# Final norm's sums and spreads among the queries' units, and five weight tiles' bounds as TensorE sums, in a fused two-block kernel

## The chip, the cores and the metric

One core of a Trainium2 chip runs the whole program in one launch. The metric is the device time of that core in microseconds (us). The kernel before takes 2531.79 us, the median of three runs from 2530.01 to 2536.81.

## The reference

The input `x` has 1024 tokens of 1024 features. A first block adds a gated mixer and a feed-forward part, and ends in a norm. A second block has differential attention, whose queries, keys, values and gates come from one projection of the normed `x`, and then a stick-breaking attention. Around the change it is this:

```python
        h = rms_norm(x, norm2_g[l])
        f = jnp.square(jax.nn.relu(jnp.einsum('bsd,df->bsf', h, w_ff1[l])))
        x = x + jnp.einsum('bsf,fd->bsd', f, w_ff2[l])
    return rms_norm(x, final_g)                       # end of the first block
...
    h = _rms(x, norm_g)                               # a_norm_2, start of the second
    proj = h @ w_in
    q, k, v, g = jnp.split(proj, [DA_QK, 2 * DA_QK, 2 * DA_QK + DA_V], axis=-1)
    qs = [_rope_partial(_rms(q[:, :, :, c], q_norm), pos) for c in range(2)]
    ks = [_rope_partial(_rms(k[:, :, :, c], k_norm), pos) for c in range(2)]
```

## The kernel before, in words

**Numbers.** Every big product is made of three float16 products (high half by high half, high by low, low by high). So every weight tile and every activation is first scaled by a power of two and split into a float16 high half and a float16 low half. The power of two comes from a bound on the tile's values.

**Weight tiles.** Tiles are numbered 0 to 41 (`TILES`). 20 and 21 are the last of the second feed-forward matrix, 22 and 23 the query columns, 24 and 25 the key columns, 26 and 27 the values, 28 and 29 the gates, 30 and 31 the output projection. A tile goes through six steps: a DMA on the SyncE queue lands it in the one raw buffer (`load(i)`, which waits until tile i-1 has been converted, `weight`); VectorE takes each partition's largest magnitude (`measure`, a reduce over 4096 elements, signal `w_peak`); GpSimd reduces that over the partitions (`across`, a `partition_all_reduce`, signal `w_top`); VectorE makes the power of two (`factor`, three tiny instructions by way of `power`, signal `w_factor`); ScalarE writes the high half (`convert`, signal `w_high`); VectorE writes the low half (`convert_low`, signal `weight`). Which step of which tile is put behind which product is written out by hand in two tables, `MEASURE[(tile in use, use)]` and `CONVERT[(tile in use, use)]`; `LOW` is one use behind `CONVERT`. `feed(i, use)` on each engine looks them up.

**Order.** Nothing is scheduled by a tool: five functions (`tensor`, `vector`, `scalar`, `gpsimd`, `sync`) write out the program of each engine in order, and semaphores tie them together. An engine's instruction that waits holds up all that stands behind it on that engine. PSUM has eight banks that `banks.take` deals out in turn, so a new bank waits until the one taken eight takes before has been emptied.

**The end of the feed-forward part.** `ff_end[2]` holds 16 products ("down" products, j = 0 to 15, 12 matmuls each). They add to the second half of the tokens (n = 1; for j = 8 to 15 this is each feature block's last addition). Behind each, VectorE adds the result to the residual, ScalarE squares it twice (once plain, once times `final_g`), and GpSimd adds the squares up (`add_square`, two adds a block).

**The two norms in one.** The final norm and `a_norm_2` follow each other. For each half n of the tokens TensorE sums the squares (`sums("final", n)`), VectorE and ScalarE make the roots (`final_factors`, `final_roots`), VectorE builds a 128 x 512 matrix of four diagonals (`diagonal`), and TensorE multiplies ones by it, which spreads a row of factors over all partitions (`spread`). There are two spreads a half: `a_norm_2` makes the normed input `h` of the projection (`final_h`, which must be there before a product of that half), `final_g` scales the residual in place (`final_x`, wanted only much later: ScalarE's `spill` writes the residual to DRAM, and that must be done before unit 16 can write over it). All diagonals share one buffer, so each waits for the spread before it.

**The queries' and keys' units.** `qk_units` are 32 units of 24 matmuls: u = 0 to 3 are tile 22 for tokens 0 to 3, 4 to 7 tile 23, 8 to 11 tile 22 for tokens 4 to 7, 12 to 15 tile 23, 16 to 23 tile 24, 24 to 31 tile 25. Per unit, ScalarE squares the product (`qk_square`), VectorE reduces, scales and norms it (`qk_norm`, four instructions), GpSimd rotates it (four instructions, signal `rotated`), and TensorE transposes the rotated unit u-3 behind the product of unit u (`qk_turn`); ScalarE and VectorE then split it (`qk_high`, `qk_low`). After the 32 units come 16 products for the values (tiles 26, 27) and 16 for the gates (28, 29).

Every instruction's line number is that of a thin wrapper (`Program`): L72 is a matmul, L75 a transpose, L81 an activation, L84 a copy on ScalarE, L93 a `tensor_tensor`, L96 a `tensor_scalar`, L101 a `scalar_tensor_tensor`, L110 a `tensor_reduce`, L113 a reciprocal, L122 GpSimd's reduce over partitions, L78 a DMA. Buffers: R are the activations, RG the raw tile and the halves of three weight tiles, PS is PSUM, dg the diagonals, scl the small columns of bounds and factors, OV and oss the squares and sums of a query unit.

## Time and profile before

| what | value |
|---|---|
| median of three runs | 2531.79 us |
| the profiled execution's own time | 2530.41 us |
| its span | 2528.6 us |
| TensorE busy | 2363.5 us, 93% of the span |
| VectorE, ScalarE, GpSimd busy | 60%, 38%, 9% |
| mean granted TensorE clock | 0.974 |
| chain that ended last, by engine | PE 76%, DVE 13%, ACT 6%, issue 3% |

The span runs from the first to the last instruction; the execution's own time has 1.8 us around it. TensorE is busy in nearly all of the span, so what a change can win is in its idle stretches. In rows, PE is TensorE's matmul, DVE VectorE, ACT ScalarE, POOL GpSimd and SPq the SyncE DMA queue. In a timeline each row has a start, a duration, the engine, line and operation, the output and inputs, and in brackets how long the engine sat idle before it and who ended that.

### The profile page before, as it was taken

The page shows a single profiled execution, that of the slowest core. Times are in us where ns is not written, and L with a number is a line of the kernel's source. Part 1 is how long each engine was busy: PE and PEld are TensorE (multiplying, and loading weights), DVE is VectorE, ACT ScalarE, POOL GpSimd, SP SyncE. Part 2 cuts the span into 40 slices and gives each one's busy share as a digit, 9 for nine tenths or more (in the row PEclk, how much of TensorE's full clock was granted, in tenths as well). Part 3 has the DMA queues.
Part 4 walks back from the last instruction along what each step waited for, and adds up shares of the span by engine and source line. Part 5 has one row for each costly group of instructions (what it writes and reads, how often), then busy time and mean ns, then how long its engine had stood idle before and what let it go on. Part 6 is the DMA issues. An engine that isn't in the chain of part 4 may idle for free.

```text
span 2528.6 us, 30214 instructions
## 1 busy us (share of the span) xinstructions
PE 2363.5 (93%) x12840; PEld 1252.4 (50%) x12840; DVE 1519.4 (60%) x1962; ACT 968.2 (38%) x1383; POOL 216.0 (9%) x263
## 2 busy tenths in 40 slices
PE   6999999999999999898999777899999998888899
PEld 4445444444444444344444455654444445666764
DVE  6898755644454455777631488965534307888862
ACT  5245334212121212323321466732323116777741
POOL 0001030000000002324201101022000000000000
PEclk9999999999999999898999899999999998999999
DMA  4010011110101010121011000021130100000021
GB/s 177 34 67 34 1 34 63 70 67 34 67 34 67 34 67 34 36 101 67 34 67 34 1 1 1 8 93 34 67 133 34 68 1 34 1 1 1 1 84 50
DMA packets 50326, 116.00 MB, mean 46 GB/s; under 512 B 2386, under 2 KB 7819, under 8 KB 49808
## 3 DMA queue, kind: packets, MB, share of 16 engines
q1 hardware_dynamic: 48456, 105.40, 11.8%
q10 hardware_dynamic: 1736, 8.68, 0.8%
q8 instruction: 101, 1.65, 0.3%
q14 instruction: 33, 0.27, 0.0%
HBM read 101.49 MB, written 12.58 MB: 45 GB/s over the span
## 4 chain that ended last, share of the span: by engine, by line
PE 76%; DVE 13%; ACT 6%; issue 3%; DMA 1%; POOL 1%; ACTq 0%; DVEq 0%; POOLq 0%
PE PS L72 72%; ACT RG L81 4%; PE PS L75 3%; DVE R L93 2%; DVE R L101 2%; DVE RG L107 2%; DVE mx L110 2%; DVE RG L101 2%; ACT OV L84 1%; DVE scl L110 1%; DMA RG<-in_a_w_in 1%; DVE RG L93 1%; DVE oss L110 1%; ACT R L81 1%; ACT OV L81 0%
## 5 line engine op out<-in xcount | busy, mean ns | idle before, releaser
L72 PE MATMUL PS<-R,RG 128*128 128x512 f16 (+1 forms) x5472 | 1167.6, 375 | 10.2 <-DVE RG L101 4.7
L72 PEld LDWEIGHTS PS<-R,RG 128*128 128x128 f16 (+1 forms) x5472 | 543.4, 103 | 631.8 <-issue 14.5
L72 PE MATMUL PS<-RG,R 128*128 128x512 f16 x2880 | 634.6, 381 | 4.5 <-DVE R L101 4.0
L72 PEld LDWEIGHTS PS<-RG,R 128*128 128x128 f16 x2880 | 282.7, 98 | 337.8 <-issue 7.5
L81 ACT ACTIVATE R<-PS,scl 128x512 f32<-128x512 f32 (+1 forms) x192 | 126.8, 687 | 716.1 <-PE PS L72 616.3
L101 DVE SCALAR_TENSOR_TENSOR R<-PS,scl,R 128x512 f32<-128x512 f32 (+1 forms) x208 | 148.7, 746 | 149.2 <-PE PS L72 124.1
L107 DVE TENSOR_TENSOR_SCAN RG<-RG 128x127 f32<-128x127 f32 (+7 forms) x128 | 168.6, 1345 | 110.4 <-ACT RG L81 110.1
L72 PE MATMUL PS<-R,OV 128*128 128x64 f32 (+2 forms) x1456 | 194.5, 286 | 34.9 <-DVE R L93 32.8
L101 DVE SCALAR_TENSOR_TENSOR RG<-RG,scl 128x4096 f16<-128x4096 f32 (+1 forms) x43 | 188.7, 4389 | 52.2 <-ACT RG L81 52.2
L72 PEld LDWEIGHTS PS<-R,OV 128*128 128x128 f32 x1456 | 180.6, 199 | 45.1 <-DVE R L93 39.3
L75 PE MATMUL PS<-ident,RG 128*128 128x128 f32 x864 | 148.5, 289 | 47.1 <-ACT OV L84 23.9
L81 ACT ACTIVATE RG<-RG,scl 128x4096 f16<-128x4096 f32 (+1 forms) x43 | 156.0, 3627 | 94.4 <-DVE scl L113 94.4
L110 DVE TENSOR_REDUCE scl<-RG 128x1 f32<-128x4096 f32 x35 | 154.4, 4413 | 62.1 <-DMA RG<-in_a_w_in 24.6
L122 POOL PARTITION_ALL_REDUCE scl<-scl x62 | 38.8, 628 | 1642.6 <-DVE scl L110 1327.8
L72 PE MATMUL PS<-R 64*128 64x512 f16 (+4 forms) x1216 | 156.7, 363 | 22.3 <-ACT RG L81 20.4
L81 ACT ACTIVATE RG<-PS,scl 128x1024 f32<-128x1024 f32 (+3 forms) x172 | 168.9, 983 | 1.8 <-PE PS L72 1.8
L104 DVE CUSTOM_DVE_ANT_0 R<-R 128x512 f32<-128x512 f32 (+1 forms) x66 | 44.3, 676 | 182.5 <-ACT R L81 182.4
L84 ACT COPY OV<-PS 128x512 f32<-128x512 f32 (+3 forms) x215 | 111.0, 516 | 109.7 <-PE PS L75 105.9
L75 PEld LDWEIGHTS PS<-ident,RG 128*128 128x128 f32 x864 | 103.0, 153 | 61.0 <-DVE RG L101 26.2
L101 DVE SCALAR_TENSOR_TENSOR R<-R,OV 128x1024 f32<-128x1024 f32 x104 | 129.3, 1278 | 1.1
L81 ACT ACTIVATE RG<-PS,mx,scl 128x128 f32<-128x128 f32 (+7 forms) x128 | 106.1, 839 | 41.5 <-DVE mx L96 40.8
L93 DVE TENSOR_TENSOR R<-PS,R 128x512 f32<-128x512 f32 (+1 forms) x96 | 65.3, 683 | 75.4 <-ACT R L81 46.0
(120 smaller groups left out, 1546.7 us busy)
## 6 DMA issues: line engine op xcount, KB each, us to landing
RG<-in_w_ff SPq DMA_DIRECT2D x16, 2048.0 KB, 8.1
RG<-in_a_w_in SPq DMA_DIRECT2D x8, 2048.0 KB, 8.5
RG<-in_w_in SPq DMA_DIRECT2D x4, 2048.0 KB, 9.6
xspill<-R ACTq DMA_DIRECT2D x2, 4096.0 KB, 15.3
RG<-in_w_kv SPq DMA_DIRECT2D x4, 2048.0 KB, 8.0
RG<-in_b_w_in SPq DMA_DIRECT2D x4, 2048.0 KB, 7.9
R<-in_x SPq DMA_DIRECT2D x8, 512.0 KB, 9.1
RG<-in_w_out SPq DMA_DIRECT2D x2, 2048.0 KB, 7.7
```

The lines of the kernel that those rows point to most:

```text
L72: return self.engine.matmul(*a, **k) if self.engine else Nothing()
L75: return self.engine.transpose(*a) if self.engine else Nothing()
L81: return self.engine.activation(*a, **k) if self.engine else Nothing()
L84: return self.engine.copy(*a) if self.engine else Nothing()
L93: return self.engine.tensor_tensor(*a) if self.engine else Nothing()
L101: return self.engine.scalar_tensor_tensor(out=out, in0=in0, scalar=scalar, in1=in1, op0=op0, op1=op1)
L104: return self.engine.tensor_tensor_reduce(*a) if self.engine else Nothing()
L107: return self.engine.tensor_tensor_scan(*a) if self.engine else Nothing()
L110: return self.engine.tensor_reduce(*a, **k) if self.engine else Nothing()
L122: return self.engine.partition_all_reduce(*a) if self.engine else Nothing()
```

## The change

1. For the first half of the tokens, the `final_g` diagonal, its spread and `final_x` leave the last down products (j = 11 to 13) and go to the queries' units 4 (diagonal), 6 (spread), 7 and 8 (`final_x`).
2. For the second half, the sums of squares move from unit 1 to 2, the `a_norm_2` spread from 2 to 3, `final_h` from units 2 and 3 (four blocks each) to 3 to 6 (two each), the `final_g` diagonal from 4 to 8, its spread from 6 to 10, `final_x` from 6, 7 to 10, 11, and the spill from 9 to 12.
3. The hand-written tables change: tile 23 is converted behind down product j = 12 instead of 8; 24 is measured behind unit 9 (before: 5) and its factor made behind 12 (6); 25 is measured behind 17 (10), factor 19 (12); 26 behind 22 (16), factor 24 (17); 27 behind 27 (24), factor 29 (25); 28 behind the values' products 1 and 3 (before 0 and 1). Low halves follow one unit later.
4. For tiles 24, 25, 26, 27 and 30, GpSimd no longer reduces the bound over the partitions. Instead TensorE multiplies a 128 x 128 matrix of ones by the column of peaks (`bound`), which leaves their sum on every partition. It takes a PSUM bank, which the first instruction of `factor` reads and frees. On TensorE the `bound` stands ahead of the product of the unit behind which VectorE makes the factor.

```diff
-for _i in (7, 8, 19, 20, 21, 22, 23, 30, 31, 32, 33, 35):
+for _i in (7, 8, 19, 20, 21, 22, 23, 24, 25, 26, 30, 31, 32, 33, 35):
     del MEASURE[_i, 1], CONVERT[_i, 2]
...
-                   (21, (19, 1), (19, 2)), (22, (19, 6), (20, 1)), (23, (20, 7), (21, 9)),
-                   (24, (23, 2), (23, 3)), (25, (22, 7), (23, 5)), (32, (30, 7), (30, 8)),
+                   (21, (19, 1), (19, 2)), (22, (19, 6), (20, 1)), (23, (20, 7), (21, 13)),
+                   (24, (22, 6), (23, 5)), (25, (24, 2), (24, 4)), (26, (24, 7), (25, 1)),
+                   (27, (25, 4), (25, 6)), (28, (26, 2), (26, 4)), (32, (30, 7), (30, 8)),
...
+BOUNDED = (24, 25, 26, 27, 30)
...
+            def bound(i):
+                b = banks.take(("bound", i))
+                e.wait_ge(*sig("w_peak").at(i))
+                e.wait_ge(*banks.free(("bound", i)))
+                e.matmul(b[:, 0:1], ones[:, :], w_col(i, 0), start=True, stop=True).then_inc(*full.up("bound", i))
+            def feed(i, use):
+                if CONVERT.get((i, use)) in BOUNDED:
+                    bound(CONVERT[i, use])
...
                 if j == 8:
                     spread("a_norm_2", 0)
-                if j == 12:
-                    spread("final_g", 0)
...
             for u, (which, c, t) in enumerate(qk_units):
-                if u == 1:
+                if u == 2:
                     sums("final", 1)
-                if u == 2:
+                if u == 3:
                     spread("a_norm_2", 1)
-                if u == 6:
-                    spread("final_g", 1)
+                if u in (6, 10):
+                    spread("final_g", u // 10)
+                feed(22 + 2 * which + c, t + 1)
                 product_n(22 + 2 * which + c, t, ("qk", u), ready=h_ready("a_norm_2", t // 4))
...
             for t in range(NT):
+                if t == 2:
+                    bound(30)
                 for c in range(2):
                     product_n(28 + c, t, ("gg", t, c))
...
             def factor(i):
+                if i in BOUNDED:
+                    key = ("bound", i)
+                    e.wait_ge(*full.at(*key))
+                    power(w_inv(i), w_col(i, 2), banks.ap(key)[:, 0:1], key=key).then_inc(*sig("w_factor").up(i))
+                    return
...
             for u in range(32):
-                if u == 1:
+                if u == 2:
                     final_factors(1)
-                    diagonal(("final_g", 0), ("a_norm_2", 1), 12)
-                if u in (2, 3):
-                    final_h(1, range(4 * u - 8, 4 * u - 4))
+                    diagonal(("a_norm_2", 0), ("a_norm_2", 1), 12)
                 if u == 4:
-                    diagonal(("a_norm_2", 1), ("final_g", 1), 4)
-                if u in (6, 7):
-                    final_x(1, range(4 * u - 24, 4 * u - 20))
+                    diagonal(("a_norm_2", 1), ("final_g", 0), 0)
+                if 3 <= u < 7:
+                    final_h(1, range(2 * u - 6, 2 * u - 4))
+                if u in (7, 8):
+                    final_x(0, range(4 * u - 28, 4 * u - 24))
+                if u == 8:
+                    diagonal(("final_g", 0), ("final_g", 1), 4)
+                if u in (10, 11):
+                    final_x(1, range(4 * u - 40, 4 * u - 36))
                 qk_norm(u)
...
             def measure(i):
+                if i in BOUNDED:
+                    return
                 e.wait_ge(*sig("w_peak").at(i))
                 across(w_col(i, 1), w_col(i, 0)).then_inc(*sig("w_top").up(i))
```

How the order moves at three places. First, TensorE at the last down products, between j = 11 and j = 12:

```order
 L72 MATMUL PS<-R,RG 128x512 [waits s_bank_dve]
 L72 MATMUL PS<-R,RG 128x512 x11
-L72 MATMUL PS<-dg,ones 128x512 [waits s_bank_dve,s_diagonal]
+L72 MATMUL PS<-R,RG 128x512 [waits s_bank_dve]
+L72 MATMUL PS<-R,RG 128x512 x11
 L72 MATMUL PS<-R,RG 128x512 [waits s_bank_dve]
 L72 MATMUL PS<-R,RG 128x512 x11
```

The spread and its wait for the diagonal are gone from among the down products; products stand next to each other.

Second, TensorE at unit 24, the first of tile 25 (`s_rotated` is GpSimd's signal, `s_w_peak` VectorE's):

```order
 L75 MATMUL PS<-ident,R 128x128 x3
 L72 MATMUL PS<-RG,R 128x512 [waits s_qk_gain]
 L72 MATMUL PS<-RG,R 128x512 x23
+L75 MATMUL PS<-ident,R 128x128 [waits s_rotated]
+L75 MATMUL PS<-ident,R 128x128 x3
+L72 MATMUL PS<-scl,ones 128x1 [waits s_qk_gain,s_w_peak]
+L72 MATMUL PS<-RG,R 128x512 [waits s_bank_dve,s_weight]
+L72 MATMUL PS<-RG,R 128x512 x23
+L75 MATMUL PS<-ident,R 128x128 [waits s_qk_gain,s_rotated]
+L75 MATMUL PS<-ident,R 128x128 x3
```

The bound of tile 26 now stands on TensorE ahead of unit 24's product, and waits there for VectorE's peaks of tile 26; before, TensorE waited for no peak.

Third, VectorE in the change, from the reduce that takes the peaks of tile 26 (behind unit 22) through unit 23 to the start of unit 24's part; the factor of tile 26 follows behind that part:

```order
L110 TENSOR_REDUCE scl<-RG 128x1 [waits s_raw]
L110 TENSOR_REDUCE oss<-OV 128x8 [waits s_qk_square]
L101 SCALAR_TENSOR_TENSOR R<-PS,scl,PB 128x512 [waits s_bank_full]
L113 RECIPROCAL orr<-orr 128x8 [waits s_qk_root,s_qk_gain]
L93 TENSOR_TENSOR R<-R,orr 128x512 [waits s_dve_step]
L93 TENSOR_TENSOR R<-PS,R 128x4x128 [waits s_qk_high]
L93 TENSOR_TENSOR scl<-scl 128x1 [waits s_weight]
L110 TENSOR_REDUCE oss<-OV 128x8 [waits s_qk_square,s_w_scale]
```

Before, this reduce of tile 26 stood behind unit 16 and its factor behind unit 17, one unit later.

## Rows read from the trace of the kernel before

**Rows 1.** The page, part 1 (busy us, share, count) and a group of part 5.

```profile
PE 2363.5 (93%) x12840; PEld 1252.4 (50%) x12840; DVE 1519.4 (60%) x1962; ACT 968.2 (38%) x1383; POOL 216.0 (9%) x263
...
L81 ACT ACTIVATE R<-PS,scl 128x512 f32<-128x512 f32 (+1 forms) x192 | 126.8, 687 | 716.1 <-PE PS L72 616.3
```

**Rows 2.** Who TensorE waited for, 1000 to 1330 us: total, times, longest.

```profile
PE PS L72 <- DVE dg L93: 12.3, 1, 12.3
PE PS L75 <- POOL R L93: 11.7, 3, 8.2
```

**Rows 3.** Timeline of TensorE, last down products to query unit 2.

```profile
1014.35 10.52 PE L72 MATMUL PS<-R,RG 128*128 128x512 f16 x48
1037.14 2.08 PE L72 MATMUL PS<-dg,ones 128*128 128x512 f32 x2 [12.27 <-DVE dg L93]
1039.01 11.41 PE L72 MATMUL PS<-R,RG 128*128 128x512 f16 x48
...
1055.44 1.84 PE L72 MATMUL PS<-ones,R 128*128 128x1 f32 x16
...
1062.33 1.02 PE L72 MATMUL PS<-dg,ones 128*128 128x512 f32 x2
```

**Rows 4.** Timeline of TensorE, query and key units.

```profile
1144.52 1.12 PE L75 MATMUL PS<-ident,R 128*128 128x128 f32 x4 [8.16 <-POOL R L93]
1145.42 7.63 PE L72 MATMUL PS<-RG,R 128*128 128x512 f16 x24
...
1183.18 0.66 PE L75 MATMUL PS<-ident,R 128*128 128x128 f32 x4 [2.05 <-POOL R L93]
1183.68 7.03 PE L72 MATMUL PS<-RG,R 128*128 128x512 f16 x24
...
1202.21 5.34 PE L72 MATMUL PS<-RG,R 128*128 128x512 f16 x24
...
1207.83 5.34 PE L72 MATMUL PS<-RG,R 128*128 128x512 f16 x24
```

**Rows 5.** Timeline of POOL: adds of squares, a reduce, rotations.

```profile
1047.48 7.40 POOL L93 TENSOR_TENSOR R<-R 128x512 f32<-128x512 f32 x6 [0.78 <-ACT R L81]
...
1218.19 0.38 POOL L122 PARTITION_ALL_REDUCE scl<-scl  x1 [5.88 <-issue]
1225.73 5.24 POOL L93 TENSOR_TENSOR OV<-R,OV 128x128 f32<-128x128 f32 x3 [7.16 <-issue]
```

**Rows 6.** Timeline of VectorE, last down products: low half, three residual additions.

```profile
1022.54 0.69 DVE L93 TENSOR_TENSOR R<-R 128x512 f16<-128x512 f32 x1 [2.73 <-ACT R L84]
1023.15 4.48 DVE L101 SCALAR_TENSOR_TENSOR RG<-RG,scl 128x4096 f16<-128x4096 f32 x1
1027.54 0.75 DVE L101 SCALAR_TENSOR_TENSOR R<-PS,scl,R 128x512 f32<-128x512 f32 x1
...
1033.72 2.76 DVE L93 TENSOR_TENSOR R<-R 128x512 f16<-128x512 f32 x2
...
1037.01 0.74 DVE L101 SCALAR_TENSOR_TENSOR R<-PS,scl,R 128x512 f32<-128x512 f32 x1
```

**Rows 7.** Timeline of VectorE among the units: `final_x`, peaks, factor, low half.

```profile
1099.64 2.70 DVE L101 SCALAR_TENSOR_TENSOR R<-R,cols,PS 128x512 f32<-128x512 f32 x4
...
1208.38 0.69 DVE L110 TENSOR_REDUCE oss<-OV 128x8 f32<-128x512 f32 x1 [2.55 <-ACT OV L81]
...
1211.21 4.41 DVE L110 TENSOR_REDUCE scl<-RG 128x1 f32<-128x4096 f32 x1
...
1218.60 0.34 DVE L96 TENSOR_SCALAR scl<-scl 128x1 f32<-128x1 f32 x2 [0.17 <-POOL scl L122]
...
1223.49 0.69 DVE L110 TENSOR_REDUCE oss<-OV 128x8 f32<-128x512 f32 x1 [4.35 <-ACT OV L81]
...
1226.32 4.47 DVE L101 SCALAR_TENSOR_TENSOR RG<-RG,scl 128x4096 f16<-128x4096 f32 x1
```

**Rows 8.** Loads of a raw tile into RG by SPq, 1000 to 1330 us.

```profile
DMA to landing us min/median/max: 7.9/8.5/19.6
```

More of the change, by code:

```diff
@@ L961, in measure, with power @@
                                 apply_absolute_value=True).then_inc(*sig("w_peak").up(i))
-            def power(inv, f, top, bits=14):
-                e.tensor_scalar(inv, top, TINY, 2.0 ** -bits, ALU.max, ALU.mult).then_inc(*step.up())
-                e.wait_ge(*step.last())
+            def power(inv, f, top, bits=14, key=None):
+                done = sig("bank_dve") if key else step
+                up = banks.empty([key], done, *key) if key else step.up()
+                e.tensor_scalar(inv, top, TINY, 2.0 ** -bits, ALU.max, ALU.mult).then_inc(*up)
+                e.wait_ge(*done.last())
                 e.tensor_scalar(inv.bitcast(I32), inv.bitcast(I32), EXPONENT, None,
@@ L1455, in vector @@
                     final_h(0, range(2 * j - 16, 2 * j - 14))
-                if j == 11:
-                    diagonal(("a_norm_2", 0), ("final_g", 0), 0)
-                if j in (12, 13):
-                    final_x(0, range(4 * j - 48, 4 * j - 44))
                 down(key, j % 8 + 9)
@@ L2101, in scalar @@
             for u in range(32):
-                if u == 1:
+                if u == 2:
                     final_roots(1)
-                if u in (2, 3):
-                    final_h(1, range(4 * u - 8, 4 * u - 4))
-                if u == 9:
+                if 3 <= u < 7:
+                    final_h(1, range(2 * u - 6, 2 * u - 4))
+                if u == 12:
                     spill()
@@ L2394, in gpsimd @@
             for t in range(NT):
-                if t == 1:
-                    measure(30)
                 gg = GG[:, t, :].rearrange("p (h e) -> p h e", h=8)
```

## The prediction

> **What bounds the kernel now.** The page comes first: TensorE is busy 93% of the span [rows 1], so a change can win no more than TensorE's idle time in its own stretch, and it loses whatever it makes TensorE wait. Second, who TensorE waited for between 1000 and 1330 us [rows 2]: only two releasers, 12.3 us once for a diagonal of VectorE and 11.7 us in three waits for GpSimd. Third, TensorE's timeline. The 12.27 us stand ahead of the `final_g` spread among the last down products [rows 3]. After them the spread's two matmuls took 2.08 us, where they take 1.02 at the full clock, and the next 48 matmuls 11.41, where 48 took 10.52: 1.95 us lost to the clock. The GpSimd waits stand ahead of transposes among the units [rows 4]: 8.16, 2.05 and, by rows 2, 1.5 us. After the 8.16 us the transposes took 1.12 us (0.66 in a milder case) and the product 7.63 against 5.34, so 2.75 us lost; after the 2.05 us the product took 7.03, so 1.7 lost. Fourth, GpSimd's timeline says why [rows 5]: its reduce over the partitions is 0.38 us long but has 5.88 us of issue ahead of it and 7.16 behind, in which nothing is rotated.
>
> **What is removed.** The spread and its diagonal leave the down products: 12.3 + 1.95. Four reduces leave GpSimd while it rotates; all three waits for it go with them: 11.7 + 2.75 + 1.7. Together 30.4 us. That is the whole gain; the rest of this part asks what is late next.
>
> The Trainium skill, GPSIMD Engine Reference (4. When to use GPSIMD), names GpSimd as the only option for a reduce over partitions. By that rule the bounds would stay there, and the sum below would lose both its 16.1 us of GpSimd waits and its 21.5 us of bounds.
>
> **Added 1: the sums of unit 2 wait for GpSimd's adds.** TensorE now runs straight on from 1024.7 us (1014.35 plus 10.5, less the last matmul's tail): four down products of 2.6 us, then two units of 5.2, so it stands at the `final` sums at 1045.4. VectorE: its residual addition for j = 9 was at 1027.54 [rows 6]. It loses tile 23's low half (4.4 us) and the 2.73 us wait for ScalarE, which was converting that tile, so it moves to 1020.4. From there to j = 11's addition were 9.5 us, less 0.6 for the diagonal (one 128x512 instruction, as from 1022.54 to 1023.15): 1029.3, done 1030.0. Now tile 23 comes in: ScalarE squares twice (0.69 each, rows 1) and converts (the 4.35 us in rows 7 hold a conversion and a square, so 3.7), VectorE's low half takes 4.4, the addition for j = 13 0.7: about 1040.1. Six adds on GpSimd for the last three blocks take 7.40 us [rows 5] and begin 0.8 later: ready at 1048.3, a wait of 2.9 us. GpSimd's three rotation instructions took 5.24 us while VectorE wrote a low half (1225.73 beside 1226.32, rows 5 and 7). If the adds for j = 12 are held up likewise until the low half ends at 1039.5, eight adds follow at 1.23: ready 1049.4, a wait of 4.0. The Trainium skill, GPSIMD Engine Reference (8. Key points), has a rule for this: GpSimd shares its SBUF interfaces with VectorE and contends with instructions of two SBUF inputs. By it the wait is the 4.0, without it 2.9; the trace leans to the rule. I take 3.5, and 2.0 for the clock (between 1.7 after 2.05 us and the 1.95 to 2.75 after the long waits). **5.5 us**, ends 0.5 and 6.8.
>
> **Added 2: TensorE waits for VectorE's peaks at its bounds.** This wait is new in kind. A unit lasts 5.62 us on TensorE (1202.21 to 1207.83, rows 4). Call F the end of a unit's product. VectorE, if not behind, begins that unit 0.83 us later (1208.38 after 1207.55), spends 2.83 on it, and then takes a tile's peaks in 4.41 [rows 7]: peaks at F + 8.1. TensorE stands ahead of the product two units on at F + 5.9 (0.28 plus 5.62). Tile 25: measured behind unit 17, bound ahead of 19, wait **2.2 us**, plus 0 to 1.7 for the clock (none seen at the 1.5 us wait); I take 3.0 in all.
>
> Tiles 26 and 27 are worse, since their raw tile must land first. From a bound that starts at 0: the bound 0.3, product 5.34, VectorE's unit 0.83 + 2.83, factor 0.54, then 4.35 in which ScalarE converts and squares, another unit 2.83, low half 4.47, issue 0.1: the next load starts at 21.6. It lands in 8.5 us [rows 8], the peaks take 4.4: 34.5. VectorE reaches this reduce earlier and waits there, so what it had to do before hides nothing. The next bound stands five units on, ahead of unit 24 and again of 29: 0.3 + 5 x 5.62 = 28.4. Wait **6.1 us, twice**. Clock after each 2.4 (between 1.95 and 2.75): 17.0 us in all. Ends: a landing of 7.9 gives 5.5, a slow 9 gives 6.6.
>
> Tile 24 (measured behind 9, bound ahead of 12) is not waited for: three units on, TensorE stands at F + 11.5. Tile 30's peaks are taken during the values, long before its bound.
>
> **Added 3: the five bounds themselves.** No such instruction is in the trace. The sums' sixteen one-column matmuls took 1.84 us [rows 3], a column (two of them) 0.23; with the column of ones to load, 0.3 each, **1.5 us**; ends 0.5 and 2.5.
>
> **Moved, at no cost.** (a) Tile 24's weight is now made behind unit 13 and wanted at unit 16. Count from the end F of unit 9's product, where VectorE has caught up: its unit and peaks 8.1; units 10 and 11 with four blocks of `final_x` each (2.7 + 2.83, rows 7) 19.1; unit 12 and factor 22.5; ScalarE 26.8; unit 13 and low half 34.1. TensorE: 0.28, six units, a spread (0.86) and a bound (0.3): 35.2. The cover is 1.1 us thin; rival B lives there. (b) The first half's `final_x` (two groups) and its diagonal are VectorE work in units 4 to 8, where a unit with a part of `final_h` (four instructions of some 0.65, rows 6) needs 5.4 us of 5.62. The last `final_x` frees its bank at 16.3 on that count; its taker, unit 13, comes at 18.3. (c) The spill goes out with the last `final_x`, at 19.1 on that count; tile 25's load follows 15 us later, and VectorE wants the spill done at unit 16, from 41 on: 22 us, more than the longest landing of a load, 19.6 [rows 8]. (d) Spreads wait for diagonals built two units earlier: nothing. (e) Tile 28's later conversion has twelve value products before the gates.
>
> **Sum.** -30.4 + 5.5 + 3.0 + 17.0 + 1.5 = **-3.4 us**. The profiled execution took 2530.41 us, 1.4 below the median of 2531.79; against it 2527.0, against the median **2528.4 us**. Own ends: 17.6 us added gives 2519, 32 gives 2533.
>
> **Rival A: the peaks are there when TensorE comes.** Then only the sums' wait and the bounds are added: -30.4 + 5.5 + 1.5 = -23.4, 2508.4 us. For it: before, peaks were ready ahead of TensorE's need. Against it: 34.5 against 28.4 us, each part from a row; it needs 6 us out of a chain in which only the landing varies, by 0.6. One of the three bounds may still be free: 2519 or so.
>
> **Rival B: VectorE is late with tile 24, slower than before.** At the last down products two half-splits beside GpSimd's adds took 2.76 us [rows 6] where two take about 1.3; 1.5 us more on a stretch of 8, or 18%. If GpSimd, freed of its reduces, is beside VectorE as much in units 9 to 13, the 34.1 us become 40.2: TensorE waits 5.0 at unit 16 and loses 2.75 on the clock. The two chains to the bounds hold about 15 us each of VectorE and grow by 2.7. Added 13.2, so +9.8: 2541.6 us. It decides from 1.1 us late, and from a cost of 3.4 us on the kernel is slower than before. Against it: a split took 0.69 with nothing beside it [rows 6], and among the units GpSimd has short rotations, not adds without a break.
>
> **How the numbers follow.** My case gets 0.66, A (whole or in part) 0.18, B 0.14, others 0.02. The range takes in my case, the half of A with one or two free bounds and the milder half of B: 2510 to 2540. About 0.3% (7.6 us) is what a measurement of this kernel can tell from no change: faster means under 2524.2. That is 0.14 from the low end of my case and A: 0.32. Slower, over 2539.4: most of B, 0.12. Within: 0.56.
>
> **What would show it.** TensorE's waits in the changed profile: no diagonal wait in the down products; no rotation wait of GpSimd's; one of 3 to 4 us on GpSimd at the sums of unit 2; one near 2 and two near 6 us ahead of one-column matmuls from `scl`, released by VectorE's reduce of RG, which itself sat idle for a DMA in the latter two. The granted clock falls to its lower level at each wait of 6. If those two waits are missing, I am wrong towards A; a wait ahead of unit 16's product says B.

## The result, and the profile after

The changed kernel takes 2538.11 us, the median of 20 runs (2534.75 to 2549.51), beside 2530.93 us for the kernel before (20 runs, 2527.37 to 2538.3). The ratio is 1.0033, with a 95% interval of 1.0021 to 1.0044: 7.2 us slower. The forecast was 2528.4 us, 3.4 us less than before, and most likely no change that can be told. The time lies inside the range given and 1.3 us under the 2539.4 us from which the forecast called the kernel slower, but twenty runs of each do tell it from no change, and it went the other way. That the range holds it is owed to the range's width.

The page after differs from [rows 1] by little: TensorE is busy seven us longer in a span five us longer. The counts say that the work is the same but for ten one-column matmuls, two for each bound; where the time went the page doesn't say.

```profile
span 2533.8 us, 30212 instructions
...
PE 2370.3 (94%) x12850; PEld 1255.7 (50%) x12850; DVE 1519.9 (60%) x1962; ACT 967.6 (38%) x1383; POOL 218.0 (9%) x258
```

The view that answers is who TensorE waited for between 1000 and 1330 us, as in [rows 2]: total, times, longest.

```profile
PE PS L72 <- DVE scl L110: 13.5, 3, 6.0
PE PS L72 <- DVE R L101: 6.3, 1, 6.3
PE PS L72 <- POOL R L93: 4.0, 1, 4.0
```

The diagonal's 12.3 us and the 11.7 us for rotations are gone. Three waits for peaks and one for the adds of squares came as forecast. The second row was not in the forecast: 6.3 us, once, for a `scalar_tensor_tensor` of VectorE. TensorE's timeline has each at its place, against [rows 3, 4]:

```profile
1012.76 1.02 PE L72 MATMUL PS<-dg,ones 128*128 128x512 f32 x2
1013.62 20.88 PE L72 MATMUL PS<-R,RG 128*128 128x512 f16 x96
...
1048.84 2.90 PE L72 MATMUL PS<-ones,R 128*128 128x1 f32 x16 [3.98 <-POOL R L93]
1051.61 7.71 PE L72 MATMUL PS<-RG,R 128*128 128x512 f16 x24
...
1076.86 1.02 PE L72 MATMUL PS<-dg,ones 128*128 128x512 f32 x2
1084.23 6.78 PE L72 MATMUL PS<-RG,R 128*128 128x512 f16 x24 [6.35 <-DVE R L101]
...
1120.22 0.28 PE L72 MATMUL PS<-scl,ones 128*128 128x1 f32 x2
1120.37 5.34 PE L72 MATMUL PS<-RG,R 128*128 128x512 f16 x24
...
1161.84 0.38 PE L72 MATMUL PS<-scl,ones 128*128 128x1 f32 x2 [2.00 <-DVE scl L110]
1162.08 7.03 PE L72 MATMUL PS<-RG,R 128*128 128x512 f16 x24
...
1197.56 0.59 PE L72 MATMUL PS<-scl,ones 128*128 128x1 f32 x2 [5.55 <-DVE scl L110]
1198.01 7.89 PE L72 MATMUL PS<-RG,R 128*128 128x512 f16 x24
...
1234.79 0.58 PE L72 MATMUL PS<-scl,ones 128*128 128x1 f32 x2 [5.98 <-DVE scl L110]
1235.23 8.05 PE L72 MATMUL PS<-RG,R 128*128 128x512 f16 x24
...
1271.64 58.65 PE L72 MATMUL PS<-RG,R 128*128 128x512 f16 x271
```

The down products run on without a gap, and the bound of tile 24 (1120.22) finds its peaks. The product of unit 6 stands still for 6.35 us.

**A measure with less scatter.** Runs of one kernel differ by 11 to 25 us, and the clock rows tell of the profiled ones that much of this comes later, in the attention (a mean granted clock of 0.90 to 0.96 between 1900 and 2300 us). In what follows the *stretch* runs from the start of the first `dg,ones` spread to the start of the run of values' products behind the last transpose of the units. In the changed kernel it is 1271.64 - 1012.76 = 258.9 us. Each stretch is read from one profiled execution, and how far it would differ in a second one was not measured. The same wait at the same place cost 0 or 1.7 us on the clock from one variant to another (last section), so a difference of 1 to 2 us between stretches counts only where its terms can be named in rows. The kernel before has these two ends:

```profile
1013.49 1.02 PE L72 MATMUL PS<-dg,ones 128*128 128x512 f32 x2
...
1265.75 79.59 PE L72 MATMUL PS<-RG,R 128*128 128x512 f16 x368
```

252.3 us, so the change adds 6.6 us in the stretch; the medians say 7.2. It balances term by term. What a wait costs on the clock is the excess of the rows behind it over their time at the full clock (1.84 us for the sums, 5.34 for a product):

| term | forecast | measured |
|---|---|---|
| diagonal's wait and clock | -14.3 | gone: -14.3 |
| waits for rotations and clock | -16.2 | gone: -16.2 |
| sums of unit 2 | +5.5 | 3.98 + 1.06 + 2.37 = +7.4 |
| bound of tile 25 | +3.0 | 2.00 + 0.10 + 1.69 = +3.8 |
| bounds of 26 and 27 | +17.0 | 5.55 + 0.31 + 2.55 and 5.98 + 0.30 + 2.71 = +17.4 |
| the bounds themselves | +1.5 (five) | 0.15 each, four in the stretch: +0.6 |
| unit 6's product | 0 | 6.35 + 1.44 = **+7.8** |
| sum | -3.4 | +6.5 |

**Theory.** Behind the forecast's error is one wait that was costed at nothing. PSUM banks are dealt in turn. The `a_norm_2` spread of unit 3 takes a bank and is read by `final_h`, in the change until unit 6. In the order of TensorE's program the takes behind it are unit 3's product, a transpose, unit 4's product, a transpose, unit 5's product, a transpose, the `final_g` spread of unit 6, and, eighth, unit 6's own product. VectorE's timeline fits: the last two reads of the spread stand behind unit 5's norm, and TensorE starts as the last one ends.

```profile
1082.17 0.74 DVE L101 SCALAR_TENSOR_TENSOR R<-R,cols,PS 128x512 f32<-128x512 f32 x1
1082.83 0.68 DVE L93 TENSOR_TENSOR R<-R 128x512 f16<-128x512 f32 x1
1083.43 0.74 DVE L101 SCALAR_TENSOR_TENSOR R<-R,cols,PS 128x512 f32<-128x512 f32 x1
```

VectorE is also late: it begins unit 5's part at 1079.35, 2.8 us behind the end of that product (1071.24 + 5.34), where the forecast counted 0.83 for a VectorE that keeps up. By the forecast's own rows (0.83 + 2.83 + 2.0 for VectorE up to its last read of the spread, 1.1 for TensorE up to unit 6) the wait is an estimated 4.5 us; the other 2 come of VectorE being behind.

**Rival.** VectorE is simply too slow in units 3 to 6, and TensorE would wait there whichever bank it took.

### The profile page after: what moved, and what is told of

The parts are those of the page before. It is cut to its first block, busy times and chain, and to the rows that moved or that the text cites. A ratio compares the mean times of both kernels' runs of the same rounds, so it can differ in the third digit from the quotient of the medians.

```text
span 2533.8 us, 30212 instructions
## 1 busy us (share of the span) xinstructions
PE 2370.3 (94%) x12850; PEld 1255.7 (50%) x12850; DVE 1519.9 (60%) x1962; ACT 967.6 (38%) x1383; POOL 218.0 (9%) x258
## 3 DMA queue, kind: packets, MB, share of 16 engines
q1 hardware_dynamic: 48456, 105.40, 11.7%
## 4 chain that ended last, share of the span: by engine, by line
PE 78%; DVE 12%; ACT 6%; issue 2%; DMA 1%; POOL 1%; ACTq 0%; DVEq 0%; POOLq 0%
PE PS L72 75%; PE PS L75 4%; ACT RG L81 3%; DVE RG L107 2%; DVE mx L110 2%; DVE R L93 2%; DVE R L101 2%; DVE RG L101 1%; DVE scl L110 1%; ACT OV L84 1%; DVE RG L93 1%; ACT R L81 1%; DMA RG<-in_a_w_in 1%; POOL R L93 1%; DVE oss L110 1%
## 5 line engine op out<-in xcount | busy, mean ns | idle before, releaser
L72 PE MATMUL PS<-R,RG 128*128 128x512 f16 (+1 forms) x5472 | 1166.3, 375 | 10.7 <-DVE RG L101 5.4
L72 PE MATMUL PS<-RG,R 128*128 128x512 f16 x2880 | 641.5, 383 | 9.9 <-DVE R L101 9.4
L75 PE MATMUL PS<-ident,RG 128*128 128x128 f32 x864 | 149.4, 290 | 46.4 <-ACT OV L84 23.9
L75 PEld LDWEIGHTS PS<-ident,RG 128*128 128x128 f32 x864 | 103.5, 154 | 60.0 <-issue 24.3
```

The source lines that it names most:

```text
L72: return self.engine.matmul(*a, **k) if self.engine else Nothing()
L75: return self.engine.transpose(*a) if self.engine else Nothing()
```

## The experiments

All ratios are to the kernel before on the same chip, worked out from all runs of both, so they are not the quotients of two medians. The median of the kernel before was 2531.89 us beside e1 to e4, 2530.72 beside e5, e6, e9 and e10, and 2528.05 beside e7, e8 and e12; medians of different groups should be compared by the ratios.

| kernel | median us (runs) | ratio, 95% interval | stretch us |
|---|---|---|---|
| changed kernel | 2538.11 (20) | 1.0033 [1.0021, 1.0044] | 258.9 |
| e1_free_bank | 2534.8 (12) | 0.9995 [0.9973, 1.0018] | 249.0 |
| e2_pool_reduces | 2518.16 (12) | 0.9956 [0.9933, 0.9979] | 240.4 |
| e3_both | 2513.08 (6) | 0.9927 [0.9899, 0.9955] | 233.3 |
| e4_bounds_spaced | 2505.93 (6) | 0.9911 [0.9884, 0.9938] | 230.7 |
| e5_tile23_early | 2507.37 (6) | 0.9928 [0.9894, 0.9962] | 231.9 |
| e6_tile23_late | 2499.33 (4) | 0.9892 [0.9857, 0.9926] | 223.2 |
| e9_spread_at_7 | 2530.49 (10) | 1.0006 [0.9985, 1.0026] | 253.2 |
| e10_spaced_gpsimd | 2515.4 (5) | 0.9937 [0.9915, 0.996] | 228.9 |
| e7_norms_alone | 2534.17 (10) | 1.0017 [0.9995, 1.004] | 251.5 |
| e8_tables_alone | 2549.88 (5) | 1.006 [1.0027, 1.0093] | 259.3 |
| e12_late_gpsimd | 2501.91 (6) | 0.989 [0.9859, 0.9921] | 221.9 |

### The bank: e1_free_bank and e9_spread_at_7

e1 takes the changed kernel and lets `final_h` finish in unit 4, on VectorE and on ScalarE alike:

```diff
-                if 3 <= u < 7:
-                    final_h(1, range(2 * u - 6, 2 * u - 4))
+                if u in (3, 4):
+                    final_h(1, range(4 * u - 12, 4 * u - 8))
```

> The changed kernel with one edit: the second half's final_h in units 3 and 4, four blocks each, instead of two each in units 3 to 6. Theory (the a_norm_2 spread of unit 3 holds its PSUM bank until the last final_h, and unit 6's product is the eighth take after it): the 6.35 us wait ahead of unit 6 and the 1.4 us of clock behind it go, -7.8 us against the changed kernel, so about 2530. Rival (VectorE is simply too late with its queue in units 3 to 8, whatever holds the bank): a wait of 3 us or more on VectorE turns up at another unit up to 10, and under 4 us are won.

The wait is gone. The same product follows the spread without a pause, and the whole list of TensorE's waits is the other two kinds:

```profile
PE PS L72 <- DVE scl L110: 13.4, 3, 5.8
PE PS L72 <- POOL R L93: 4.0, 1, 4.0
```

```profile
1077.79 1.02 PE L72 MATMUL PS<-dg,ones 128*128 128x512 f32 x2
1078.65 5.34 PE L72 MATMUL PS<-RG,R 128*128 128x512 f16 x24
```

The stretch falls by 9.9 us: 7.8 for the wait and its clock, and 1.7 because the product behind the 1.99 us wait at tile 25's bound now ran in 5.34 us. Of the whole time 3.3 us show in the medians and 9.6 in the two ratios (1.0033 and 0.9995). e1's profiled execution had a granted clock of 0.92 between 1900 and 2300 us, the changed kernel's 0.96, in a part that the edit does not touch. But e1 gives VectorE four blocks in each of two units in place of two in each of four, so it moves VectorE's work as well as the bank. e9 leaves VectorE's program alone and moves one spread on TensorE:

```diff
-                if u in (6, 10):
+                if u in (7, 10):
                     spread("final_g", u // 10)
```

> The changed kernel with TensorE's first final_g spread moved from ahead of unit 6 to ahead of unit 7; VectorE's program is untouched. Theory (the bank): the 6.35 us wait ahead of unit 6's product is for the PSUM bank that the a_norm_2 spread of unit 3 holds until the last final_h. Banks are dealt in turn; with the spread one unit later, the held bank falls to the taker behind that product, the transpose at its end, some 5.3 us later on TensorE, so the wait shrinks to between 0 and 1.5 us, and the stretch falls from 258.9 by 6 to 8 us to about 252. Rival (VectorE is simply late with its work in units 3 to 6, whoever asks for it): the same 6 us wait stays ahead of unit 6 or stands ahead of unit 7, and the stretch stays within 1.5 us of 258.9.

The wait changed its instruction, as the bank's turn demands: with no spread ahead of unit 6, the eighth take is the transpose behind unit 6's product.

```profile
1081.87 5.34 PE L72 MATMUL PS<-RG,R 128*128 128x512 f16 x24
1089.33 0.63 PE L75 MATMUL PS<-ident,R 128*128 128x128 f32 x4 [2.12 <-DVE R L101]
```

The 2.12 us are a little over the 1.5 that I had allowed. I forgot that the spread's own 0.86 us now stands behind the wait and not ahead of it: 6.35 - 5.18 (the product) + 0.86 = 2.03. Unit 6's product itself waits for nothing, which the rival excludes. The stretch falls by 5.7 us (forecast 6 to 8): 5.6 at the bank, 1.7 of clock behind tile 25's bound as in e1, and 1.7 given back at the sums (0.9) and at the bounds of 26 and 27 (0.8). With VectorE's program unchanged, the wait went to whoever came eighth: that the bank is what TensorE waits for is shown.

### Who should reduce the bounds: e2, e3, e4, e10

e2 is the changed kernel with the bounds of tiles 24 to 27 on GpSimd again, at the changed places. Only tile 30 keeps its TensorE sum.

```diff
-BOUNDED = (24, 25, 26, 27, 30)
+BOUNDED = (30,)
```

> The changed kernel with the bounds of tiles 24 to 27 reduced by GpSimd again, all table positions as in the change (tile 30 stays a TensorE sum). Theory (TensorE waits at its own bounds for VectorE's peaks, and at these positions GpSimd's reduce would delay no rotation that TensorE needs): the three waits for the peaks (2.0, 5.55, 5.98 us) and their clock losses (1.7, 2.6, 2.7) go and no wait for GpSimd's rotations comes: -20 to -21 us, about 2517. Rival (the late tables are the cause, not who reduces): TensorE then waits as long for rotations or for a tile's weight, and under 5 us are won.

The stretch falls by 18.5 us and the run by about 20 (19.5 by the ratios). All three waits for peaks go, and of the waits for rotations that the kernel before had only one is there, of 2.6 us (transposes are L75):

```profile
PE PS L72 <- DVE R L101: 6.3, 1, 6.3
PE PS L72 <- POOL R L93: 4.0, 1, 4.0
PE PS L75 <- POOL R L93: 2.6, 1, 2.6
```

So the reduces did not have to leave GpSimd for its waits to go: with the changed tables all but 2.6 of the 11.7 us are gone with the reduces still there. e3 has e1's edit and e2's together.

> Both edits (final_h in units 3 and 4, GpSimd's reduces for tiles 24 to 27). Theory: they add, -28 to -29 us against the changed kernel, about 2509.5, which is 21 under the kernel before. Rival: with TensorE 8 us earlier, tile 24's weight (1 us of slack) or the spill is late, and 5 us or more come back as a wait near unit 16.

233.3 us, 25.5 below the changed kernel, where the two alone give 9.9 + 18.5 = 28.4. Of the 2.9 between them 1.7 is the clock behind tile 25's bound, which both take away. e4 keeps the sums on TensorE and e1's `final_h`, but places them so that the peaks are ready: tile 25 is measured one unit sooner, the factors of 26 and 27 are made one and two units later (27 is measured one later), and 28 and 29 follow.

```diff
-                   (24, (22, 6), (23, 5)), (25, (24, 2), (24, 4)), (26, (24, 7), (25, 1)),
-                   (27, (25, 4), (25, 6)), (28, (26, 2), (26, 4)), (32, (30, 7), (30, 8)),
+                   (24, (22, 6), (23, 5)), (25, (24, 1), (24, 4)), (26, (24, 7), (25, 2)),
+                   (27, (25, 5), (25, 8)), (28, (26, 5), (26, 6)), (29, (27, 3), (27, 4)), (32, (30, 7), (30, 8)),
...
-LOW[36, 1], LOW[31, 1] = 37, 32
+LOW[36, 1], LOW[31, 1], LOW[26, 1] = 37, 32, 27
```

> final_h in units 3 and 4 and all bounds on TensorE, but the chain from one bound to the next gets six units instead of five: tile 25 measured behind unit 16 instead of 17, 26's factor behind 25 instead of 24, 27's behind 31 instead of 29 (measured behind 28), 28 and 29 five and two products later. Theory (a chain of 34.5 us against units of 5.62 us): the waits at the bounds shrink from 2.0, 5.6 and 6.0 us to at most 0.7 each without a loss of clock, so -26 us against the changed kernel, about 2512. Rival (the bound costs by itself, or VectorE's own place in the order is what TensorE waits for): two or more waits over 2 us stay.

The waits at the bounds shrink from 13.5 us to 1.0, none with a loss of clock behind it, and the stretch is 230.7 us. e10 asks whether TensorE's sums are worth having at these places; it is e4 with `BOUNDED = (30,)`.

> e4_bounds_spaced with the bounds of tiles 24 to 27 reduced on GpSimd again, at the same spaced places; only tile 30 keeps its TensorE sum. Theory: in the changed tables the bounds on TensorE cost because of who is waited for, not by themselves: at the spaced places the TensorE sums wait 1.0 us in all and cost 0.28 us each. GpSimd's reduces, with 5.9 us of issue ahead of them and 7.2 behind, hold up the rotations by 2.6 to 2.9 us once at the changed places; here I expect one or two waits for a rotation, of 1 to 3 us each, and a stretch 0 to 4 us longer than e4's 230.7. Rival: GpSimd's reduces cost nothing once they are far from the factor, so TensorE's bounds (1.1 us of matmul, 1.0 of wait) are pure loss and the stretch is 1 to 2 us shorter than 230.7.

By the stretch they are not. It is 1.9 us shorter still, the rival's 1 to 2, and 1.6 of it can be named: 1.0 us of waits and four sums of 0.15 us are saved, and no transpose waits for a rotation. Whole runs do not show this: e10's median is 9.5 us above e4's, its lowest run 1.0 below, and the intervals of the two ratios overlap. e10's profiled execution had a granted clock of 0.91 between 1900 and 2300 us, e4's 0.96; whether that is chance, no run settles. TensorE's whole list has one row. GpSimd's timeline in e10 shows that a reduce there costs what it did in [rows 5] (6.35 us ahead of it, in part the wait for the peaks, 7.14 behind it), only that nobody stands at the transposes meanwhile: three units' rotations then follow at once.

```profile
PE PS L72 <- POOL R L93: 4.0, 1, 4.0
```

```profile
1220.95 0.38 POOL L122 PARTITION_ALL_REDUCE scl<-scl  x1 [6.35 <-DVE scl L110]
1228.47 1.06 POOL L93 TENSOR_TENSOR OV<-R,OV 128x128 f32<-128x128 f32 x3 [7.14 <-issue]
```

What made the 8.16 us wait of [rows 4], then? I had not looked at what VectorE did ahead of it. In the kernel before, VectorE did nothing for 11.18 us behind unit 10, at tile 25's peaks, since the load had not landed, and unit 11, whose transposes are the ones that wait, stood behind it. SyncE issued that load at 1111.65 and ScalarE the spill of 4 MB at 1112.32. That is the one load that took 19.6 us [rows 8]. The spill was held up too: it landed in 17.4 us, and in 13.0 or 13.1 in the changed kernel and in every variant, where no load was issued beside it.

```profile
1131.25 4.42 DVE L110 TENSOR_REDUCE scl<-RG 128x1 f32<-128x4096 f32 x1 [11.18 <-DMA RG<-in_a_w_in]
```

```profile
1111.65 0.37 SPq L78 DMA_DIRECT2D RG<-in_a_w_in  x1
```

```profile
1112.32 0.37 ACTq L78 DMA_DIRECT2D xspill<-R  x1
```

GpSimd had its part, behind the peaks:

```profile
1135.81 0.38 POOL L122 PARTITION_ALL_REDUCE scl<-scl  x1 [14.71 <-DVE scl L110]
1142.93 1.00 POOL L93 TENSOR_TENSOR OV<-R,OV 128x128 f32<-128x128 f32 x3 [6.74 <-issue]
```

TensorE stood at the transposes from 1136.36 on, and VectorE had unit 11 ready at 1138.48. Two estimates from these rows part the causes. Without the reduce and the 6.74 us behind it, the rotation (1.5 us) ends at 1140.0 and TensorE waits 3.7 us, not 8.16. With the reduce but with a load of 8.5 us, the peaks are there at 1124.6, the reduce runs at 1127.0 (5.9 us of issue behind GpSimd's last rotation), the next rotation ends near 1136.1, and nobody waits. So the late load is what the wait needed, and GpSimd's round trip made it twice as long.

In the changed kernel the spill goes out at 1124.62, the next load at 1141.79, and no load of a raw tile between 1000 and 1330 us lands later than 8.8 us:

```profile
DMA to landing us min/median/max: 7.7/8.4/8.8
```

e7, below, parts load and spill with the table of before.

### The sums of unit 2: e5_tile23_early and e6_tile23_late

Both are e4 with another place for tile 23, whose conversion and low half stand in the last down products. e5: behind j = 8, as in the kernel before.

```diff
-                   (21, (19, 1), (19, 2)), (22, (19, 6), (20, 1)), (23, (20, 7), (21, 13)),
+                   (21, (19, 1), (19, 2)), (22, (19, 6), (20, 1)), (23, (20, 7), (21, 9)),
```

> e4_bounds_spaced with one number changed: tile 23 is converted behind down product j = 8 again, as in the kernel before. Theory: the 4.0 us wait of TensorE ahead of the sums of unit 2 exists because ScalarE's conversion and VectorE's low half of tile 23 stand between the last residual additions and GpSimd's last eight adds. With them four products earlier the adds begin some 3 us sooner and are not held up under the low half (some 9.9 us for eight in place of 14.1), so the wait goes wholly, with the 3.4 us that the clock gave back after it: the stretch from the first spread to the 72-us run of value products is 23.5 in the units of the other stretches less, 230.7 - 7 = about 224 us, and the run about 2499. Rival 1: four products earlier the low half delays the diagonal or the residual additions of j = 9 to 11 and makes a new wait among the down products of 2 us or more; then the stretch stays above 228. Rival 2: it is GpSimd's eight adds alone that are late, whoever is beside them; then a wait of 2 us or more stays at the sums.

The theory fell here. The wait at the sums stays, as rival 2 had it, and another came among the down products, as in rival 1 but shorter (1.2 us); the stretch is 231.9 us:

```profile
PE PS L72 <- POOL R L93: 3.7, 1, 3.7
PE PS L72 <- DVE R L101: 1.2, 1, 1.2
```

VectorE's low half stands ahead of the last residual additions at either place and delays them at either: the last one ended 27.8 us after the start of the stretch in the changed kernel and 26.3 after it in e5. In e5 the last five came in one go at 1036.62 us, and GpSimd then had ten adds to do, not eight. They took 1.28 us each, but began 24.4 us after the start of the stretch, where the changed kernel's eight began 21.9 after it:

```profile
1036.62 3.37 DVE L101 SCALAR_TENSOR_TENSOR R<-PS,scl,R 128x512 f32<-128x512 f32 x5
```

```profile
1038.09 12.77 POOL L93 TENSOR_TENSOR R<-R 128x512 f32<-128x512 f32 x10 [1.95 <-ACT R L81]
```

e6 puts both steps behind the last addition: conversion behind j = 15, low half behind unit 0.

```diff
-                   (21, (19, 1), (19, 2)), (22, (19, 6), (20, 1)), (23, (20, 7), (21, 13)),
+                   (21, (19, 1), (19, 2)), (22, (19, 6), (20, 1)), (23, (20, 7), (21, 16)),
...
-LOW[36, 1], LOW[31, 1], LOW[26, 1] = 37, 32, 27
+LOW[36, 1], LOW[31, 1], LOW[26, 1], LOW[22, 1] = 37, 32, 27, 23
```

> e4_bounds_spaced with tile 23 converted one product later than the last addition (behind down product j = 15) and its low half behind unit 0. Theory: as in e5, the last eight adds of GpSimd are no longer behind the conversion nor under the low half, so the 4.0 us wait at the sums of unit 2 and its 3.4 us of clock go: stretch about 224 us, run about 2499. Rival 1: the low half, 4.5 us of VectorE behind unit 0, comes too late for unit 4, the first of tile 23, or pushes the diagonal for unit 3; then a wait of 1 us or more stands at unit 3 or 4 and the gain is under 5 us. Rival 2: the adds alone are late; a wait of 2 us or more stays.

Now the theory holds to a us (forecast 224, measured 223.2). In TensorE's rows the sums follow at the full clock, and the only wait left in the list is 0.5 us at tile 27's bound. The last residual addition ended 22.5 us after the start of the stretch, and GpSimd's ten adds began 17.2 after it:

```profile
1045.66 1.84 PE L72 MATMUL PS<-ones,R 128*128 128x1 f32 x16
1047.36 5.34 PE L72 MATMUL PS<-RG,R 128*128 128x512 f16 x24
```

```profile
1030.92 12.33 POOL L93 TENSOR_TENSOR R<-R 128x512 f32<-128x512 f32 x10 [1.96 <-ACT R L81]
```

### The two halves of the change: e7_norms_alone and e8_tables_alone

e7 has the norm's new places (parts 1 and 2) with the tables and GpSimd reduces of before; e8 has the tables and TensorE bounds (parts 3 and 4) with the norm of before. In e7 the edit of the changed kernel is

```diff
-BOUNDED = (24, 25, 26, 27, 30)
+BOUNDED = ()
```

with the old table and tile 30's reduce back on GpSimd; in e8 the order of the norm in `tensor`, `vector` and `scalar` is put back.

> Parts 1 and 2 of the change alone: the norm's sums, spreads, final_h and final_x as in the changed kernel, but the tables of the kernel before and every bound reduced on GpSimd. Theory: the 12.3 us diagonal wait and its 1.95 of clock go; the sums' wait on GpSimd comes (with tile 23 converted early it was 3.7 us and 1.2 among the down products in e5), about 8 with its clock; the wait for the held bank ahead of unit 6 comes and is longer than the changed kernel's 6.35, since VectorE also takes tile 24's peaks (4.4 us) behind unit 5: 8 to 11 us; GpSimd's waits at the transposes, 11.7 in the kernel before, stay in part. Stretch 252.3 - 14.3 + 8 + 10 to 13 = 256 to 259 us, run 2534 to 2538. Rival: the bank wait hides GpSimd's first wait (8.16 at the transpose of unit 8 or so), so the two don't add up, and the stretch is 248 to 251.

251.5 us, the rival's 248 to 251 nearly. The bank wait is there and longer, as the theory wanted (10.7 us, with tile 24's peaks of 4.41 us ahead of the last `final_h`), but GpSimd's waits fell to 4.2 us. Not, or not alone, for the reason that the rival gave: tile 25's load and the spill, 0.67 us apart before, were issued at 1115.92 and 1137.86. The same load now landed in 8.7 us, and VectorE took its peaks with no wait for a DMA ahead of it, where it had stood 11.18 us. The 8.16 us wait ahead of unit 11's transposes is not in this list; the later two are. The last row is the bank once more, at the other long-held spread: the transposes behind unit 9's product are the eighth take after the `final_g` spread of unit 6, and begin as the last `final_x` of that spread ends (1115.82 + 2.71).

```profile
1130.13 4.41 DVE L110 TENSOR_REDUCE scl<-RG 128x1 f32<-128x4096 f32 x1
```

```profile
PE PS L72 <- DVE R L101: 11.9, 2, 10.7
PE PS L75 <- POOL R L93: 4.2, 2, 3.1
PE PS L72 <- POOL R L93: 3.7, 1, 3.7
PE PS L75 <- DVE R L101: 1.8, 1, 1.8
...
1118.67 0.63 PE L75 MATMUL PS<-ident,R 128*128 128x128 f32 x4 [1.80 <-DVE R L101]
```

> Parts 3 and 4 of the change alone: the changed tables and TensorE bounds on the norms of the kernel before. Theory: GpSimd's 11.7 us of waits and 4.5 of clock go; the three waits at the bounds come as in the changed kernel (13.5, with clock some 20); no wait for a held bank, since final_h stays in units 2 and 3 with four blocks each; the diagonal wait at j = 12 shrinks by the low half and the conversion that no longer stand ahead of it (12.3 to about 5), and a wait of 5 to 8 us for GpSimd's adds comes at the sums, now ahead of unit 1. Stretch 252.3 - 16.2 + 21 - 7 + 8 = 254 to 260 us. Rival: tile 23's late conversion costs more at these norms than I count (final_x stands between the additions too), sums wait over 12 us, stretch over 262.

259.3 us, as expected, and each wait of the expectation is in the list:

```profile
PE PS L72 <- DVE scl L110: 13.5, 3, 5.8
PE PS L72 <- POOL R L93: 5.1, 1, 5.1
PE PS L72 <- DVE dg L93: 5.1, 1, 5.1
```

Alone the halves move the stretch by -0.8 and +7.0 us, together by +6.6. That they nearly add up is, as far as the rows tell, chance: each alone already parts the load from the spill, and each brings a wait that the other does not have.

### The best of it: e12_late_gpsimd

e6 with `BOUNDED = (30,)`.

> e6_tile23_late with the bounds of tiles 24 to 27 reduced on GpSimd again. Theory, from e10 beside e4 (228.9 against 230.7 in the stretch): at late and spaced places GpSimd's reduces hold up no transpose, so the TensorE sums and what is waited at them are pure cost, and the stretch falls from 223.2 to about 221.5 us, the run to about 2497. Rival: with the 4 us wait at unit 2 gone, TensorE stands at every transpose 7 us earlier, and GpSimd's slack is used up: one or two waits of 1 us or more for a rotation come, and the stretch is 223 or longer.

The stretch is 221.9 us (theory 221.5, rival 223 or more), and TensorE's list is one row of 0.2 us for a rotation. Of the 1.3 us between e6 and e12 the rows name 0.9: 0.5 of wait and 0.6 of sums saved, 0.2 of wait added. In whole runs e12 and e6 can't be told apart (0.989 and 0.9892). Both beat the kernel before by 1.1% and the changed kernel, by the two ratios to the kernel before, by 1.4%.

## Why the prediction failed

- **Moved, at no cost, (b)** is the step that failed. It put the second half's `a_norm_2` spread at nothing. It asked of the last `final_x` whether its bank is free for the next taker, and did not ask it of that spread, whose reader the change had stretched over four units. The walk is the same: eight takes on from the spread of unit 3 stands unit 6's product, 6.35 us ahead of VectorE's last read. With the measured term, 7.8 us, the forecast would have been -3.4 + 7.8 = +4.4 us, 2536.2. e1 and e9 show it. The other 2.2 us up to the measured 6.6 are sizes: +1.9 at the sums, +0.8 at tile 25, +0.4 at 26 and 27, -0.9 at the bounds themselves.
- **What is removed** had the right size, 30.4 us, and half the wrong reason. "Fourth, GpSimd's timeline says why" was a reading of the last link. The largest GpSimd wait began with a load beside the spill, 11.18 us on VectorE, and went in e7 with the table and the reduces of before; e2, e3, e10 and e12 let GpSimd reduce and wait 0 to 2.9 us. GpSimd's issue time behind the reduce made that wait longer, but did not begin it. The view that I had not opened was VectorE's timeline ahead of that transpose. The forecast's own terms already had part 4 as a loss, 21.5 us paid at the bounds for 16.1 saved; what the view would have shown is that most of the 16.1 could be had without it. At the places tried, part 4 is a cost: 18.5 us in the changed tables, 1.3 to 1.9 at the spaced ones, the latter by single profiles. TensorE sums in the tables of the kernel before were not run.
- That also weighs on the sentence on the Trainium skill, GPSIMD Engine Reference (4. When to use GPSIMD). TensorE does this sum, 0.28 us a row, so GpSimd isn't the only option for it. What I worked out from the rule was that leaving the bounds on GpSimd would give up 16.1 us and spare 21.5, 5.4 us to the good. e2 left them there and the stretch was 18.5 us shorter, since only 2.6 us of GpSimd's waits came back.
- **Added 1** was right in kind, 3.98 us against 3.5, close to the 4.0 of the variant in which the low half holds GpSimd up: eight adds took 14.1 us in the changed kernel, where a low half of 4.49 us lies beside them, and ten took 12.3 in e6, where none does, so the eight took 4.2 us more than at e6's pace. This speaks for the rule of the Trainium skill, GPSIMD Engine Reference (8. Key points), on the shared interface. Its clock was taken too low: 3.4 us, not 2.0.

```profile
1034.69 14.10 POOL L93 TENSOR_TENSOR R<-R 128x512 f32<-128x512 f32 x8 [2.24 <-ACT R L81]
```

- **Added 2**: 2.00, 5.55 and 5.98 us against 2.2, 6.1 and 6.1. The chain of load, peaks and units was worked out well, and the clock signs came: the granted clock was 0.50, the lower of its two levels (1.2 of 2.4 GHz), from 1197.56 to 1200 and from 1234.79 to 1239, behind the two long waits. VectorE's reduce sat idle for the DMA ahead of both, 2.48 and 2.84 us, as the last part said.
- **Added 3**: 1.5 us against 0.75. A one-column sum takes 0.15 us of TensorE's time, from 1120.22 to 1120.37; the rest of its row lies beside the next product.
- **Moved (a), (c), (d), (e)** hold: no wait at unit 16, at the spill, at a spread or at the gates. Behind the gates, outside the stretch, the changed kernel waits 1.45 us for ScalarE ahead of the first product of the attention, the kernel before does not; no run looks into it.
- **Rival A** is not what the change does, and e4 shows what it takes to have it: peaks one unit sooner or bounds one to two units later. **Rival B** did not come: nothing waits for tile 24. Its time, 2541.6, is near the measured one by another mechanism.

## What to carry to other kernels

When a reader of a buffer that is dealt in turn is moved or spread out, count the takes from that buffer to its next taker; do it for every buffer that the edit holds longer, not for the last one alone. When a profile names the engine that was waited for, follow that engine back through its own inputs before giving it the blame; a DMA collision two engines away can stand behind it. And when work on an engine delays what somebody waits for, moving it to an earlier place in the same chain can give nothing (e5); behind the last instruction that is waited for it is out of the way (e6).

## What the runs showed that I had not expected

- What a wait of 2 us costs on the clock is not fixed. In the changed kernel and in e8 the product behind the wait of 2.00 or 1.99 us took 7.03 and 7.00 us; in e1 and e9, behind the same 1.99 us at the same place, 5.34. Behind 3.96 to 3.98 us the sums and the product lost 3.4 us in the changed kernel and in e4 (3.23 + 7.37) and 4.3 in e9 (3.57 + 7.92), and behind 10.67 us in e7 the product took only 7.67, 2.3 us lost. The longer wait isn't the dearer one.
- Two transfers, 2 MB in and 4 MB out, issued 0.67 us apart: the first landed in 19.6 us, where the same load in e7, 22 us away from the spill, took 8.7; the second landed in 17.4, alone in 13.0.
- Runs of one kernel scatter by up to 25 us: e2's lie between 2512.27 and 2537.59. In a stretch whose rows are compared one by one, terms of 1 us can be named that the medians of six runs do not show; the price is that each is seen in one execution.
